# A feed-forward layer as seven block products for eight, with up first and down in four blocks through DRAM

## What is computed

```python
def finish_layer(x, a_heads, m_out, lam_init, attn_out_norm, w_out, norm_ffn, w_up, w_down):
    ...
    x = x + jnp.concatenate([a.astype(x.dtype), m_out.astype(x.dtype)], axis=-1) @ w_out
    hf = rms_norm(x, norm_ffn) @ w_up                   # w_up (2048, 8192)
    return x + jnp.square(jax.nn.relu(hf)) @ w_down     # w_down (8192, 2048)
```

## Time and profile before

| what | us |
|---|---|
| median of 3 runs | 3805.63 |
| lowest, highest | 3805.61, 3812.92 |
| span of the profiled execution, which is also its time | 3805.8 |
| output projection, TensorE's matmuls | 2024.8 to 2220.2 |
| feed-forward stage, first to last matmul | 2226.35 to 3785.66 |
| last stage, transposes | 3788.8 to 3797.8 |

### The profile page before, as it was taken

The page is one execution under the profiler, slowest core; times in us unless marked ns, Lnnn a source line. Parts: engine busy times, 40 slices in busy tenths (PEclk is TensorE's granted clock), DMA queues, the critical chain, the costliest instruction groups (busy, mean ns, idle before and its releaser), DMA issues. The chain is left out here.

```text
span 3805.8 us, 65517 instructions
## 1 busy us (share of the span) xinstructions
PE 3571.4 (94%) x26210; PEld 3317.2 (87%) x26210; DVE 1762.8 (46%) x2737; ACT 1299.2 (34%) x1953; POOL 679.0 (18%) x431
## 2 busy tenths in 40 slices
PE   7999998875897999999988999999999999999998
PEld 7999997554746888888868999999999999999998
DVE  4222223764556777777774343333333333333333
ACT  3111111332125777777773231222221222221222
POOL 0000000000004888888850000000000000000000
PEclk9999999767978999999998999999999999999999
DMA  7433442106637999999975322222222222222221
GB/s 209 113 109 105 112 113 88 52 22 211 152 127 260 332 333 331 336 331 331 332 274 159 88 78 89 88 83 86 89 89 89 89 84 83 89 89 89 89 86 62
DMA packets 458084, 568.51 MB, mean 149 GB/s; under 512 B 41250, under 2 KB 331984, under 8 KB 457812
## 3 DMA queue, kind: packets, MB, share of 16 engines
q1 hardware_dynamic: 457812, 564.64, 46.1%
HBM read 518.08 MB, written 46.49 MB: 148 GB/s over the span
## 5 line engine op out<-in xcount | busy, mean ns | idle before, releaser
L71 PE MATMUL f_acc<-xf_hi,ffn_hi 128*128 128x272 f32 x2048 | 594.4, 290 | 0.0
L69 PE MATMUL f_acc<-hidden_hi,ffn_lo 128*128 128x272 f32 x2048 | 591.6, 289 | 2.8 <-DVE mix_t L2467 2.8
L71 PE MATMUL f_acc<-hidden_hi,ffn_hi 128*128 128x272 f32 x2048 | 592.8, 289 | 0.0
L69 PE MATMUL f_acc<-xf_hi,ffn_lo 128*128 128x272 f32 x2048 | 591.4, 289 | 0.5
L70 PE MATMUL f_acc<-hidden_lo,ffn_hi 128*128 128x272 f32 x2048 | 590.7, 288 | 0.0
L70 PE MATMUL f_acc<-xf_lo,ffn_hi 128*128 128x272 f32 x2048 | 588.7, 287 | 0.0
L1695 POOL TENSOR_TENSOR dc_vl<-dc_vpages,dc_vh 128x1024 fp32r<-128x1024 f32 x241 | 573.6, 2395 | 12.0 <-ACT dc_vh L2034 11.7
L2418 ACT ACTIVATE ffn_hi<-ffn_raw 128x2048 fp32r<-128x2048 f32 x127 | 242.3, 1908 | 619.3 <-PE f_acc L71 619.3
L69 PE MATMUL z_acc<-xn_hi,win_lo 128*128 128x280 f32 (+1 forms) x1536 | 446.2, 290 | 1.1 <-DVE win_lo L303 1.1
L71 PE MATMUL z_acc<-xn_hi,win_hi 128*128 128x280 f32 (+1 forms) x1536 | 446.7, 291 | 0.0
L70 PE MATMUL z_acc<-xn_lo,win_hi 128*128 128x280 f32 (+1 forms) x1536 | 445.5, 290 | 0.0
(11 more groups left out here) (375 smaller groups left out, 6197.3 us busy)
## 6 DMA issues: line engine op xcount, KB each, us to landing
dc_kpages<-in_cache_k SPq DMA_DIRECT2D x256, 512.0 KB, 5.4
dc_vpages<-in_cache_v SPq DMA_DIRECT2D x256, 512.0 KB, 5.2
ffn_raw<-in_w_up SPq DMA_DIRECT2D x64, 1024.0 KB, 6.3
ffn_raw<-in_w_down SPq DMA_DIRECT2D x64, 1024.0 KB, 5.0
win_raw<-in_w_in SPq DMA_DIRECT2D x48, 1024.0 KB, 6.3
ffn_raw<-in_w_out SPq DMA_DIRECT2D x16, 1024.0 KB, 6.2
z_scratch<-z_out SPq DMA_DIRECT2D x48, 280.0 KB, 2.1
sm_c<-in_state_C SPq DMA_DIRECT2D x32, 256.0 KB, 6.6
```

The costliest lines, as they stand in the source:

```text
L69: nc.tensor.matmul(out, wlo, xhi, start=first, stop=False)
L71: return nc.tensor.matmul(out, whi, xhi, start=False, stop=last)
```

## The change

`mlp` and `emit` are replaced by one stage, `feed_forward`. It computes all of `w_up` first and then all of `w_down`, in 64 units: 32 up (`PAIRS`), each of two tiles of hidden features, and 32 down, each of two output tiles for a quarter of the hidden features. In a unit the weights are a 2 by 2 of blocks (two column tiles f, two halves v of the contraction, 8 k each) and so are the activations (two halves v, two token halves). The unit forms seven products of sums of these blocks in place of eight plain ones, by Winograd's form of Strassen's scheme:

- Weights: four sums of 128x1024 (`sum1` to `sum4`, VectorE). Seven blocks of 128x1024 are split (`high` on ScalarE, `low` on VectorE), in a ring of three tiles `whi`, `wlo`; `high` of product g waits until TensorE has finished product g - 3.
- Activations: seven operands of 128x2176 (`xh`, `xl`, 8 k of 272 each). For the up phase four of them are plain (`plain`) and three are sums, made once, in the stage's beginning, by four additions on GpSimd. Unit 0 uses the plain ones and is made of eight products (four steps of 48 matmuls), while the sums are made.
- Output: products 0 to 6 go to three PSUM banks; some add to what is there. ScalarE copies three intermediate states (`hold`) and the first output block (`take21`) out, and VectorE adds three outputs (`join`).
- Up: ReLU and square on ScalarE, then GpSimd makes four differences of 272 columns, and SyncE stores seven combined hidden tiles to DRAM (`hq_dram`). The norm's factor is applied to the operand before the first product (`norm`), no longer to the hidden values.
- Down: at the borders (units 32, 40, 48, 56) the seven operands are loaded from DRAM (1088 KB each, `operand`) into `xl` and split there (`op_high`, `op_low`). The outputs are added by GpSimd to a running sum that is loaded from and stored to DRAM in each unit (`acc_dram`); in the last 8 units VectorE adds it (`finish`), and TensorE's transposes of `emit` follow at once (`turn`), one unit behind, with ScalarE's copies and SyncE's stores.
- The output projection gets buffers of its own, its first loads for the feed-forward stage are 2 MB, and it stores each residual tile (`keep`).

TensorE's program has the same three passes per product and k. The core of the diff:

```diff
...
+            for n in range(N - GROUP):
+                sp.wait_ge(flow.lo_made, n + 1)
+                sp.dma_start(tile(flow.raw, n % GROUP), w[:, :, (n + GROUP) * P:(n + GROUP + 1) * P])\
+                    .then_inc(flow.landed[n % GROUP], 16)
+                if n >= 2:
+                    keep(n - 2)
...
+        source = lambda u, i: (kv(u, 0)[:, 0], kv(u, 1)[:, 0], kv(u, 0)[:, 1], kv(u, 1)[:, 1])[i] if u == 0 else \
+            (kv(u, 0)[:, 0], kv(u, 1)[:, 0], kv(u, 0)[:, 0], total[:, :, :], kv(u, 0)[:, 1], kv(u, 1)[:, 0],
+             kv(u, 1)[:, 1])[i]
...
+            def operand(u, i):
+                sp.wait_ge(used, step(u, i) + 1)
...
+                sp.dma_start(xl[:, i, :, :].bitcast(F32).rearrange("p k t -> p (k t)"), hqx[b][HQ[i]]).then_inc(op_in[i], 16)
...
+            T(xn(1, 1), xn(1, 1), xn(0, 1), ALU.subtract).then_inc(t_made, 1)
+            pool.wait_ge(t_made, 1)
+            T(xn(0, 1), xn(0, 1), xn(0, 0), ALU.subtract).then_inc(t_made, 1)
...
+            for u in range(PAIRS):
+                z = piece(u)
+                pool.wait_ge(squared, u + 1)
+                T(z[:, 4, :], z[:, 1, :], z[:, 0, :], ALU.subtract).then_inc(combined, 1)
...
+            for u in range(PAIRS, LAST):
...
+                T(tops(u), tops(u), z, ALU.add).then_inc(added, 1)
...
+            def high(u, i):
+                g = step(u, i)
+                if g >= 3:
+                    act.wait_ge(used, g - 2)
...
+            for u in range(1, UNITS):
+                for i in range(STEPS):
+                    high(u, i)
+                    if i == 2 and u >= 2:
+                        take21(u - 1)
+                    if i == 3:
+                        hold(u, 0, 0, 0, s1)
+                        if 2 <= u <= PAIRS:
+                            relu_square(u - 1)
+                    if i == 5:
+                        hold(u, 1, 0, 2, s2)
+                    if i == 6:
+                        hold(u, 2, 2, 3, s5)
...
+                    if last_of_block(u) and i == 5:
+                        op_high(u, 0)
+                    if last_of_block(u) and i == 6:
+                        op_high(u, 1)
+                    if first_of_block(u) and i <= 4:
+                        op_high(u - 1, i + 2)
...
+            for u in range(1, UNITS):
+                for i in range(STEPS):
+                    if i == 0 and u >= 2:
+                        join(u - 1, 3, 2, 0, 4, s5, c22)
+                    low(u, i)
+                    if i == 0:
+                        sum2(u)
+                    if i == 1:
+                        sum4(u)
+                        if u >= 2:
+                            join(u - 1, 1, 1, 2, 5, s2, c12)
+                    if i == 3 and u > LAST:
+                        finish(u - 1)
+                    if i == 4:
+                        join(u, 0, 0, 1, 1, s1, c11)
+                    if i == 5 and u + 1 < UNITS:
+                        sum1(u + 1)
+                    if i == 6 and u + 1 < UNITS:
+                        sum3(u + 1)
...
+                    if last_of_block(u) and i == 6:
+                        op_low(0, STEPS * block_of(u + 1) + 1)
+                    if first_of_block(u) and i <= 5:
+                        op_low(i + 1, STEPS * block_of(u) + i + 2)
...
+                    if first_of_block(u):
+                        pe.wait_ge(op_lo, STEPS * block_of(u) + i + 1)
...
+                    if i in (2, 4, 5):
+                        pe.wait_ge({2: s1, 4: s2, 5: s5}[i], u)
+                    if i == 6:
+                        pe.wait_ge(c22, u)
+                    out = b[(0, 1, 0, 2, 0, 2, 0)[i]][:, 0:H]
+                    for k in range(KH):
+                        mm = exact_passes(nc, out, whi[:, g % 3, k, :], wlo[:, g % 3, k, :], xh[:, i, k, :],
+                                          xl[:, i, k, :], k == 0 and i in (0, 1, 3), k == KH - 1, i not in (0, 1, 3))
+                    mm.then_inc(used, 1)
...
```

More of the change, by code:

```diff
@@ new lines, in feed_forward @@
+        extra = [ctx.enter_context(nc.psum_tensor(f"ff_extra{i}", [P, 512], F32)) for i in range(2)]
+        flat = mix[:, :, :].rearrange("p k t -> p (k t)")
+        late = flat[:, 0:4096].rearrange("p (j n) -> p j n", j=2)
+        area = [flat[:, 4096 + r * 8 * H:4096 + (r + 1) * 8 * H] for r in range(2)]
+        spare = flat[:, 4096 + 16 * H:4096 + 16 * H + 512]
+        assert d.kc * d.t >= 4096 + 16 * H + 512
+        root = held[:, 0:2, :].rearrange("p h t -> p (h t)")
+        xn = lambda k2, h, ks=slice(0, 8): mix[:, ks.start + k2 * KH:ks.stop + k2 * KH, N_META + h * H:N_META + (h + 1) * H]
@@ new lines, in _ @@
+            sp.wait_ge(lo_made, 3)
+            weights(1, 0)
+            sp.wait_ge(lo_made, 4)
+            weights(1, 1)
+            sp.wait_ge(t_lo, 4)
+            sp.wait_ge(t_made, 4)
+            weights(2, 0)
+            weights(2, 1)
+            for u in range(1, UNITS):
+                turn = last_of_block(u)
+                if u == PAIRS:
+                    keep_hidden(u - 1)
+                if u >= PAIRS:
+                    load_top(u)
+                if PAIRS < u <= LAST:
+                    keep_top(u - 1)
+                if turn:
+                    operand(u, 0)
+                    operand(u, 1)
+                if u < PAIRS and not turn:
+                    more(u, 0)
+                    keep_hidden(u - 1)
+                    more(u, 1)
+                elif turn:
+                    more(u, 0)
+                    operand(u, 2)
+                    if u < PAIRS:
+                        keep_hidden(u - 1)
+                    operand(u, 3)
+                    more(u, 1)
+                    for i in range(4, STEPS):
+                        operand(u, i)
+                else:
+                    more(u, 0)
+                    more(u, 1)
+                if u > LAST:
+                    send(u - 1)
@@ L2428, in run @@
-            def run(g, first):
-                for i in range(2 * G):
-                    if not (first and i < 2):
-                        split(g, i, first)
-                    if 1 <= i <= G:
-                        hidden(g, i - 1)
-            act.wait_ge(flow.gain_in, 16)
-            for k in range(d.kc):
-                nc.scalar.activation(xhi[:, k, :], xt[:, k, :], ACT.Copy, scale=flow.gain[:, k:k + 1]).then_inc(x_hi, 1)
-            act.wait_ge(shifted, 1)
-            nc.scalar.activation(root[:, :], root[:, :], ACT.Sqrt).then_inc(rooted, 1)
@@ new lines, in _, with high_t @@
+            for i in range(3):
+                high(0, i)
+            act.wait_ge(shifted, 2)
+            A(root, root, ACT.Sqrt).then_inc(rooted, 1)
+            for k in range(d.kc):
+                act.wait_ge(normed, k + 1)
+                A(plain(xh, k), row(k)).then_inc(x_hi, 1)
+                if k == 11:
+                    high(0, 3)
+            def high_t(op, place, n):
+                act.wait_ge(t_made, n)
+                if op == 6:
+                    act.wait_ge(used, 3)
+                A(xh[:, op, :, :], place).then_inc(t_hi, 1)
@@ L2475, in run @@
-            def run(g, first):
-                for i in range(2 * G):
-                    if not (first and i < 2):
-                        split(g, i)
-                    if i == 0 and not first:
-                        add(g - 1, G - 1)
-                    if 1 <= i <= G:
-                        hidden(g, i - 1)
-                    if i > G:
-                        add(g, i - G - 1)
-            nc.vector.memset(over[:, :], 1.0 / d.dm).then_inc(over_made, 1)
-            dve.wait_ge(flow.gain_in, 16)
@@ L2495, in _, with low @@
-            split(0, 1)
-            dve.wait_ge(rooted, 1)
-            nc.vector.reciprocal(rstd[:, :], root[:, :]).then_inc(inverted, 1)
-            dve.wait_ge(inverted, 1)
-            groups(dve, run)
-            add(GROUPS - 1, G - 1)
+            V = nc.vector
+            def low(u, i):
+                g = step(u, i)
+                dve.wait_ge(hi_made, g + 1)
+                V.tensor_tensor(wlo[:, g % 3, :, :], source(u, i), whi[:, g % 3, :, :].bitcast(F32),
+                                ALU.subtract).then_inc(lo_made, 1)
```

542 lines of the change are left out of this document (332 added, 210 removed).

## The result

The changed kernel takes **3694.42 us**, the median of 4 runs from 3691.62 to 3699.57; the kernel before, on the same chip, 3807.05 (4 runs, 3805.61 to 3812.92). The ratio is 0.9698, with a 95% interval from 0.9683 to 0.9712. The forecast was 3705 us in 3650 to 3785. The profiled execution took 3696.74 us, with a span of 3695.0.

The account below looks back on a forecast made before the run. TensorE, busy for 94% of the span, was taken as the bound, so only fewer matmuls could help. Start 2320 + middle units 1314.5 + borders 52 + transposes 7.7 + end 11.5 = 3705.7, forecast 3705 us, range 3650 to 3785.

Parts of the forecast that it names:

- transposes: 80 transposes placed between the last units' products, seven eighths of their 8.93 us on TensorE's path: 7.7 us.
- after the last product: From the last product to the span's end: copy, sum, ten transposes, three copies and stores, 11.5 us, bounds 9 and 15.
- all low bounds: The forecast's sum with every step at its low bound, given as 3651 us.
- the two rivals priced by it: GpSimd's 176 us delays TensorE in every unit: 40% of it gives 3776 us (chance 0.15), all 3882 us (0.06).
- A unit in the middle: 62 units of 168 matmuls, bound by TensorE at 21.2 us each, 1314.5 us in all; other engines stay under that.
- The two tight waits: In middle units, product 2 on ScalarE's hold and product 6 on VectorE's join, both met by over 1 us.
- the slower one: Rival: in all 63 units every GpSimd instruction holds up the split TensorE waits for, 176 us, 3882 us; chance 0.06.
- It doesn't do what it says: Rival: fewer matmuls, but their interval rises to 0.1444 us with VectorE's load, about 3806 us and more; chance 0.02.
- GpSimd in VectorE's way: VectorE instructions with two SBUF inputs and GpSimd's exclude each other; 3.1 us a middle unit, costed at nothing there.
- The start: Stage's beginning through unit 1: norm, splits, GpSimd's sums alternating with VectorE until 2298; ends at 2320, bounds 2299 and 2335.
- The borders: Before units 32, 40, 48, 56: VectorE 11 us over, ScalarE and landings 2; 13 each, 52 in all, bounds 32 and 88.
- The side work is free: Rival: splits at the borders and GpSimd's sums overlap, start ending at 2299, borders 32 us: 3665 us; chance 0.11.

Follow-up runs that it names:

- edit 9: Changed kernel with the four operand sums of the start made by VectorE in place of GpSimd; median of 4 runs 3689.45 us, ratio 0.9681.
- e_both: Changed kernel with the four operand sums on VectorE and a border's operands issued by SyncE ahead of the weights; median of 5 runs 3685.91 us, ratio 0.9673.
- e_weights_last: Changed kernel with SyncE issuing a border's operands ahead of the next weights and, before the first border, the hidden tiles' store; 3693.49 us, ratio 0.9695.

## Why the prediction was right

The forecast was 10.6 us too high against the median. Two terms were mis-sized (the start, and the two parts of the borders, whose errors nearly cancel). By its steps, against the profiled execution (span 3695.0):

| step | predicted | measured |
|---|---|---|
| end of unit 1 | 2320 | 2313.5 |
| 62 units | 1314.5 | 1313.8 |
| four borders | 52 | 49.3 |
| transposes | 7.7 | 7.5 |
| after the last product | 11.5 | 10.9 |
| sum | 3705.7 | 3695.0 |

The end of unit 1 is the third hold of unit 2 (2326.66), less the hold's 1.0 us behind its product and four products of 3.03. The transposes are seven units by 1.07. The last term is what is left. Two figures of the prediction don't come out of its own terms: all low bounds give 3662, not 3651, and GpSimd adds in 24 of the 32 down units, so its whole time is 156 us, not 176, and the two rivals priced by it would stand at 3768 and 3862. Neither touches the forecast.

*A unit in the middle, 21.2 us*: right, to 0.01 us. The two tight waits, with just over 1 us of room each by the working, never showed, and even with GpSimd's differences doubled no matmul in the middle was late. With this the two rivals that made each unit pay fall, the slower one above all: its exclusion of the engines is real, but it did not reach TensorE. That the three weight buffers absorb it is the prediction's reading; no run has fewer.

*It doesn't do what it says*: refuted by the interval, 0.1261 us with VectorE at 72%.

*GpSimd in VectorE's way* (with the Trainium skill's "SBUF — State Buffer", "Who interferes with whom"): right, and confirmed more sharply than the rows before could. An instruction of 1.22 us took 4.89 to 5.85 us beside one of 4.87. The trace agrees with this rule of the Trainium skill. The prediction drew the right price from it, but didn't ask the next question: whether GpSimd should do this work at all, since a lock makes the slower engine's time come on top. That is what edit 9 is worth, some 7 us.

*The start* is the step that was mis-sized, 6.5 us too long, although the stage began 2.6 us later than in the profile before (first instruction at 2227.31 for 2224.76). The alternation was priced rightly: all of it was put to end at 2298, and the last split of an operand ended at 2297.06. Behind it the prediction put 22 us (evacuation of unit 0, its own splits, weights that load only then, three products, 3 us for the clock) one after another; 16.4 were needed. Two windows, one ahead of that split and one behind it:

```profile
2286.00:2290.00 4.00, 3.50 (x15) 3.50 (x16) 3.90 (x3) 3.18 (x4) 0.00 (x0) 0.50 0.00 0
2297.06:2313.50 16.44, 12.40 (x97) 12.02 (x96) 10.24 (x10) 8.08 (x12) 3.89 (x4) 1.00 0.97 300
```

The lower clock came while the alternation still ran, and was over behind it: there the term of 3 us was worth nothing. The rest lies in loads, evacuation and products, which overlap in part. How much each gives was not tried.

*The borders*: 49.3 for 52, inside the bounds of 32 and 88, and VectorE's splits are a limit at each, as said. What was wrong is the form of the working: 11 us for VectorE plus 2 for ScalarE and landings. The waits came to 34.6 us, 8.7 a border, and the lower clock after them to 14.6, 3.7 a border, for which the prediction had a place only in its upper bound. So that 52 and 49.3 are so near is partly luck: a term 4 us too high a border, and one that was missing. VectorE's work and the landings don't add either. The landing is a second limit almost as long, some 3 to 4 us less than the first at units 40 and 48 (7.3 and 6.7 left with the splits halved, 1.7 and 1.6 with the loads halved too), and 12.3 us from issue to landing is not the 3.4 that came of the attention stage's 334 GB/s: in this stretch the queue was at 420 GB/s and the engines' share at 1.01, with 2 MB of weights and, at unit 32, some 1.9 MB of stores ahead or between. *The side work is free*: refuted by the borders and the start.

## What to carry to other kernels

Where two engines exclude each other on SBUF, moving work to the slower one does not relieve the faster one: add both times, and where the sum is on the path, give the work to the faster engine. A stall can have two limits of like length, and then a remedy for one alone can measure as nothing (ratio 0.9695 for 0.9698 here), so halve suspected costs singly and together before judging. Part each stall into idle time and matmuls at the lower clock: here 34.6 and 14.6 us, and the second went away only when the waits were short. When single runs differ by more than the effect, count from time stamps inside the stage and not from the total.

## What the runs showed of the hardware

- Two engines that lock each other don't just alternate: the profile shows each instruction's wait as its duration, so VectorE's 1.22 us read as 5.8 and GpSimd's 4.87 as 5.7.
- Doubling GpSimd's work in the middle raised VectorE's busy time by 46 us in 600 and slowed no matmul there.
- The loads of 1.1 MB at a border, which compete with weights and stores, took 12.3 us to land (median), halved loads 7.2 to 8.3; at full size but issued ahead of the weights they took 7.7. 1 MB of weights had taken 5.0 to 6.3 in the kernel before. What stood ahead in the queue counted as much as the size.
- Two kernels with the same 8.2 us of idle time at a border (unit 32 in `e_both` and `e_weights_last`) lost 9.5 and 12.2 us there, with a granted clock of 1.00 and 0.95 over the stretch.
- The same program ahead of the stage reached it 10 us apart in single executions, more than most of the effects that were looked for.
